# Decays of a gated recurrence as running products, scores in four pieces, and outputs with tokens in the partitions

## The reference

```python
f = lb + (1.0 - lb) * jax.nn.sigmoid(f_pre)
log_f = jnp.log(f)
k = 1.0 - f
...
def step(state, xs):
    qc, lfc, kc, vc = xs
    b = jnp.cumsum(lfc, axis=2)
    o_inter = jnp.einsum('bhtk,bhkv->bhtv', qc * jnp.exp(b), state)
    diff = b[:, :, :, None, :] - b[:, :, None, :, :]
    decay = jnp.exp(jnp.where(causal, diff, -jnp.inf))
    attn = jnp.einsum('bhtk,bhsk,bhtsk->bhts', qc, kc, decay)
    o_intra = jnp.einsum('bhts,bhsv->bhtv', attn, vc)
    b_last = b[:, :, -1, :]
    k_dec = kc * jnp.exp(b_last[:, :, None, :] - b)
    new_state = jnp.exp(b_last)[..., None] * state + jnp.einsum('bhsk,bhsv->bhkv', k_dec, vc)
    return new_state, o_inter + o_intra
...
o = rms_norm(o, hgrn_norm_w[l]) * jax.nn.silu(heads(g_h, HGRN_HEAD_V))
```

## Time and profile before

| | before |
|---|---|
| median of 3 runs | 1179.38 us (1178.89 to 1179.52) |
| the profiled execution: time, span | 1178.28 us, 1176.5 us |
| PE busy | 1125.3 us, 96% |
| DVE, ACT, POOL busy | 73%, 47%, 14% |
| granted clock of PE, mean | 0.99 |
| DMA, mean | 116 GB/s |

### The profile page before, as it was taken

How to read it: one execution, slowest core, us unless ns; L and a number is a source line. 1 busy time by engine, 2 the same in 40 slices (tenths; PEclk the granted TensorE clock), 3 DMA queues, 4 the chain that set the end, 5 groups by cost and what they waited for, 6 DMA issues and landing times.

```text
span 1176.5 us, 15092 instructions
## 1 busy us (share of the span) xinstructions
PE 1125.3 (96%) x5995; PEld 902.4 (77%) x5995; DVE 859.3 (73%) x1348; ACT 554.4 (47%) x857; POOL 164.6 (14%) x179
## 2 busy tenths in 40 slices
PE   4889999999999999999999999999999999999996
PEld 3667777777788878888886766778888888888885
DVE  5879899999867784666788799786765666655246
ACT  3574555544622343776425676546544434341130
POOL 1044443334423210000100000200000000000001
PEclk9899999999999999999999999999999999999999
DMA  9642323323524566313110022112333233243201
GB/s 376 250 179 99 117 77 139 143 74 142 172 88 171 204 260 233 116 64 121 52 38 37 1 72 72 36 72 72 108 108 103 77 108 106 79 158 141 91 17 71
DMA packets 22654, 136.66 MB, mean 116 GB/s; under 512 B 2576, under 2 KB 2872, under 8 KB 8760
## 3 DMA queue, kind: packets, MB, share of 16 engines
q1 hardware_dynamic: 19936, 128.46, 30.0%
q10 hardware_dynamic: 2648, 7.25, 1.8%
HBM read 133.58 MB, written 2.12 MB: 115 GB/s over the span
## 4 chain that ended last, share of the span: by engine, by line
PE 68%; DVE 18%; ACT 6%; issue 3%; POOL 3%; DMA 2%; DVEq 0%; SPq 0%; ACTq 0%; POOLq 0%
PE PB L185 67%; DVE WL L206 3%; DVE RAW L1412 3%; ACT WH L199 2%; DVE AT L234 1%; DVE UPA L206 1%; DVE SS L214 1%; POOL UPA L206 1%; POOL PTA L206 1%; DVE PTA L206 1%; DVE MPH L1412 1%; DVE XL L214 1%; DMA XL<-in_x 1%; DMA RAW<-in_wstream 1%; DVE HB L231 1%
## 5 line engine op out<-in xcount | busy, mean ns | idle before, releaser
L185 PE MATMUL PB<-HH,WH 128*128 128x512 f32 (+1 forms) x896 | 352.9, 394 | 12.1 <-DVE HL L206 7.4
L185 PE MATMUL PB<-HH,WL 128*128 128x512 f32 (+1 forms) x896 | 340.7, 380 | 0.0
L185 PE MATMUL PB<-HL,WH 128*128 128x512 f32 (+1 forms) x896 | 340.4, 380 | 0.0
L206 DVE TENSOR_TENSOR WL<-RAW,WH 128x1024 fp32r<-128x1024 f32 (+2 forms) x172 | 205.5, 1201 | 178.9 <-ACT WH L199 178.6
L199 ACT ACTIVATE WH<-RAW 128x1024 fp32r<-128x1024 f32 (+2 forms) x172 | 167.4, 979 | 290.9 <-PE PB L185 265.3
L185 PEld LDWEIGHTS PB<-HH,WH 128*128 128x128 f32 x896 | 169.3, 189 | 49.8 <-DVE HL L206 8.4
L185 PEld LDWEIGHTS PB<-HH,WL 128*128 128x128 f32 x896 | 169.4, 189 | 32.9
L185 PEld LDWEIGHTS PB<-HL,WH 128*128 128x128 f32 x896 | 169.7, 189 | 28.6 <-issue 0.5
L214 DVE SCALAR_TENSOR_TENSOR CV<-VP,PC,CV 128x512 f32<-128x512 f32 x120 | 88.1, 778 | 0.7
L206 POOL TENSOR_TENSOR PX<-PX,NPOW 128x2 f32<-128x2 f32 (+2 forms) x7 | 6.5, 935 | 461.2 <-DVE PX L206 422.8
L185 PE MATMUL PB<-WH,AH 128*128 128x512 f32 x176 | 68.5, 389 | 0.0
(11 more groups left out here) (283 smaller groups left out, 1789.3 us busy)
## 6 DMA issues: line engine op xcount, KB each, us to landing
RAW<-in_wstream SPq DMA_DIRECT2D x101, 1024.0 KB, 4.9
EARLY<-in_wstream SPq DMA_DIRECT2D x7, 1024.0 KB, 15.8
RAW<-in_wstream SPq DMA_DIRECT2D x5, 768.0 KB, 4.5
RAW<-in_wstream SPq DMA_DIRECT2D x5, 512.0 KB, 3.6
XL<-in_x SPq DMA_DIRECT2D x2, 1024.0 KB, 8.5
HB<-in_x SPq DMA_DIRECT2D x2, 1024.0 KB, 6.3
out<-XL SPq DMA_DIRECT2D x8, 256.0 KB, 2.0
ROWS<-in_rows ACTq DMA_DIRECT2D x3, 512.0 KB, 8.1
```

The costliest lines, as they stand in the source:

```text
L185: return self.put(lambda e: e.matmul(o, l, r, start=start, stop=stop, skip_group_check=skip))
L206: return self.put(lambda e: e.tensor_tensor(o, a, b, op))
```

## The change

No logarithm, scan or exponential is left. ACT makes both f (into Bb) and k (into Kb) from the sigmoid with two linear activations (`gates`). The decays are built up level by level, in place: `Kb` and a working copy of the queries `QM` (Qb times f; two buffers, the former Q0 and E0) hold the decays within blocks of 2^(l-1) tokens; DVE's `up(l)` multiplies the earlier halves of Kb by the gate product of the later half, and the later halves of QM by that of the earlier half, two instructions of 256 columns. POOL makes those products of 2, 4, ... 64 gates by pairs (`total`, into TOT: 256, 128, ... 8 columns). ACT copies, at each level, the early halves of Kb and the late halves of QM into EW[l-1] (two instructions). So level l+1 can't be made before level l was copied. Scores of a level have only the 32 late tokens of each chunk as columns, and two levels share a bank and a tick: level 0 at step -3, levels 1 and 2 at step 1, 3 and 4 at step 3, 5 and 6 at step 5. After level 6 Kb and QM are the fully decayed keys and queries, used by `kt` (step 6) and `qs`. Values are turned over at step -6 instead of 0, KDT is copied by ACT at step 7, `o` and `kv` move to step 8. The output has tokens in the partitions: AT and QM are stationary, Vb and SS move; the `qs` products have 128x64 stationary tiles and 128 columns, even and odd chunks in other halves of the partitions. The square sums come from ACT's accumulator, four squares of 128 columns (step 13), so `st` on PE is gone; `dg` now multiplies XT by DG in four products of 128 columns, which scales and turns the head back, and one DVE instruction multiplies by weight and output gate. The four-instruction diagonal, the state chain, the masks and everything after the recurrence stay.

```diff
+    QM = [Q0[:, :], E0[:, :]]
...
+    PIECE = (0, 1, 1, 2, 2, 3, 3)
+
+    def totals(h, l):
+
+        if l == 1:
+            return head_bufs(h)[2]
+        if l == 7:
+            return TOT[:, 496 + 8 * (h % 2):504 + 8 * (h % 2)]
+        return TOT[:, 512 - (1024 >> (l - 1)):512 - (512 >> (l - 1))]
+
+    def pairs_of(h, l):
+        return totals(h, l).rearrange("p (n b) -> p n b", b=2)
...
-        def ew(h, l):
-            half, blk = 1 << (l - 1), 1 << l
-            Bb = head_bufs(h)[2]
-            x = ew_buf(h, l - 1)
-            Bv, Xv = halves_of(l, Bb, x)
-            ref = Bv[:, :, half - 1:half].broadcast_to([128, 512 // blk, half])
-            g.wait_ge(S_.v_s, ("b", h))
-            if ew_before(h, l - 1):
-                g.wait_ge(S_.p_sm, ew_before(h, l - 1))
-            g.tt(Xv[:, :, half:blk], Bv[:, :, half:blk], ref, SUB)
-            g.tt(Xv[:, :, 0:half], ref, Bv[:, :, 0:half], SUB).then_inc(S_.g_s, ("ew", h, l))
+        def total(h, l):
+
+            f = pairs_of(h, l - 1)
+            if l == 2:
+                g.wait_ge(S_.a_s, ("k", h))
+                if h:
+                    g.wait_ge(S_.v_s, ("uq", h - 1, 7))
+            else:
+                g.wait_ge(S_.g_s, ("tot", h, l - 1))
+            if l == 7 and h > 1:
+                g.wait_ge(S_.v_s, ("ss", h - 2))
+            g.tt(totals(h, l), f[:, :, 0:1].rearrange("p n b -> p (n b)"), f[:, :, 1:2].rearrange("p n b -> p (n b)"), MUL)\
+                .then_inc(S_.g_s, ("tot", h, l))
 
         def hgrn(h, step):
             Vb, Kb, Bb, Qb, Gb = head_bufs(h)
-            if step == -1:
+            if step == -7:
+                for l in (2, 3, 4):
+                    total(h, l)
+            elif step == -6:
+                for l in (5, 6, 7):
+                    total(h, l)
+            elif step == -5:
                 clear(h)
-            if step < 0:
-                ew(h, step + 7)
-            elif step == 3:
-                x = ew_buf(h, 6)
-                Bv, Xv = halves_of(6, Bb, x)
-                g.wait_ge(S_.p_sm, ew_before(h, 6))
-                g.tt(Xv, Bv[:, :, 63:64].broadcast_to([128, 8, 64]), Bv, SUB).then_inc(S_.g_s, ("kd", h))
             elif step == 14:
                 sc = sct(h % 2)
-                g.wait_ge(S_.v_ax, ("st", h))
+                g.wait_ge(S_.v_s, ("st", h))
                 power(sc[:, 4:8], sc[:, 0:4], 4, ("pow", h))
-            elif step == 22:
-                g.wait_ge(S_.v_ax, ("dg", h))
-                g.wait_ge(S_.a_ev, ("z", h, 3))
-                g.tt(XT[:, h, :], XT[:, h, :], Gb, MUL).then_inc(S_.g_s, ("oh", h))
...
-            if step < 0:
-                x = ew_buf(h, step + 6)
-                a.wait_ge(S_.g_s, ("ew", h, step + 7))
-                a.act(x, x, ACTF.Exp).then_inc(S_.a_s, ("ew", h, step + 7))
-            elif step == 3:
-                a.wait_ge(S_.v_s, ("b", h))
+            if -3 <= step < 3:
+                l = step + 4
+                half, blk = 1 << (l - 1), 1 << l
+                Kv, Qv, Xv = halves_of(l, Kb, QM[h % 2], EW[l - 1])
                 if h:
-                    a.wait_ge(S_.v_s, ("ss", h - 1))
-                a.act(E0[:, :], Bb, ACTF.Exp).then_inc(S_.a_s, ("e0", h))
-                x = ew_buf(h, 6)
-                a.wait_ge(S_.g_s, ("kd", h))
-                a.act(x, x, ACTF.Exp).then_inc(S_.a_s, ("kd", h))
+                    a.wait_ge(S_.p_sm, ("sc", h - 1, PIECE[l]))
+                a.wait_ge(*((S_.v_s, ("uk", h, l)) if l > 1 else (S_.a_s, ("k", h))))
+                a.copy(Xv[:, :, 0:half], Kv[:, :, 0:half]).then_inc(S_.a_s, ("xk", h, l))
+                a.wait_ge(S_.v_s, ("uq", h, l))
+                a.copy(Xv[:, :, half:blk], Qv[:, :, half:blk]).then_inc(S_.a_s, ("xq", h, l))
+            elif step == 7:
+                a.wait_ge(S_.p_sm, ("kt", h))
+                if h:
+                    a.wait_ge(S_.p_sm, ("kv", h - 1))
+                a.copy(KDT[:, :], aux.of(("kt", h))).then_inc(S_.a_ax, ("kt", h))
             elif step == 13:
                 a.wait_ge(S_.p_sm, ("qs", h))
                 a.wait_ge(S_.v_h, ("h", 7))
                 a.copy(XT[:, h, :], aux.of(("o", h)))
-                a.wait_ge(S_.v_s, ("b", min(h + 1, 7)))
-                a.act(XR[3], aux.of(("o", h)), ACTF.Square).then_inc(S_.a_ax, ("o", h))
+                for j in range(4):
+                    op = a.act(XR[3][:, js(j)], aux.of(("o", h))[:, js(j)], ACTF.Square, acc=sct(h % 2)[:, 8 + j:9 + j])
+                op.then_inc(S_.a_ax, ("o", h))
...
+            a.act(Kb, main.of(("z", h, 1)), ACTF.Sigmoid).then_inc(S_.a_ev, ("z", h, 1))
+            a.wait_ge(S_.v_s, "lb")
+            a.wait_ge(S_.a_ev, ("z", h, 1))
+            a.act(Bb, Kb, ACTF.Identity, bias=LB[:, h:h + 1], scale=OML[:, h:h + 1])
+            a.act(Kb, Kb, ACTF.Identity, bias=OML[:, h:h + 1], scale=LT[:, h:h + 1]).then_inc(S_.a_s, ("k", h))
...
-        def head(h, b):
-            Vb, Kb, Bb, Qb, Gb = head_bufs(h)
-            if b == 1:
-                v.wait_ge(S_.a_ev, ("z", h, 1))
-                v.wait_ge(S_.v_s, "lb")
-                v.ts(Kb, Kb, OML[:, h:h + 1], LB[:, h:h + 1], MUL, ADD).then_inc(S_.v_s, ("f", h))
-                v.wait_ge(S_.a_s, ("ln", h))
-                v.ts(Kb, Kb, -1.0, 1.0, MUL, ADD).then_inc(S_.v_s, ("k", h))
-                if h > 1:
-                    v.wait_ge(S_.a_s, ("kd", h - 2))
-                v.scan(Bb, SM[:, :], XR[3]).then_inc(S_.v_s, ("b", h))
-
         def hgrn(h, step):
             Vb, Kb, Bb, Qb, Gb = head_bufs(h)
-
-            def ew(l):
-                half, blk = 1 << (l - 1), 1 << l
-                Kv, Qv, Xv = halves_of(l, Kb, Qb, ew_buf(h, l - 1))
-                v.wait_ge(S_.a_s, ("ew", h, l))
-                v.wait_ge(S_.a_ev, ("z", h, 2))
-                v.wait_ge(S_.v_s, ("k", h))
-                v.tt(Xv[:, :, half:blk], Xv[:, :, half:blk], Qv[:, :, half:blk], MUL)
-                v.tt(Xv[:, :, 0:half], Xv[:, :, 0:half], Kv[:, :, 0:half], MUL).then_inc(S_.v_s, ("ew", h, l))
+            Qm = QM[h % 2]
+
+            def up(l):
+
+                half, blk = 1 << (l - 2), 1 << (l - 1)
+                Kv, Qv = halves_of(l - 1, Kb, Qm)
+                f = pairs_of(h, l - 1)
+                n = 512 // blk
+                if l == 2:
+                    v.wait_ge(S_.p_sm, ("sc", h, 0))
+                else:
+                    v.wait_ge(S_.g_s, ("tot", h, l - 1))
+                    v.wait_ge(S_.v_s, ("uq", h, l - 1))
+                v.wait_ge(S_.a_s, ("xk", h, l - 1))
+                v.tt(Kv[:, :, 0:half], Kv[:, :, 0:half], f[:, :, 1:2].broadcast_to([128, n, half]), MUL).then_inc(S_.v_s, ("uk", h, l))
+                v.wait_ge(S_.a_s, ("xq", h, l - 1))
+                v.tt(Qv[:, :, half:blk], Qv[:, :, half:blk], f[:, :, 0:1].broadcast_to([128, n, half]), MUL)\
+                    .then_inc(S_.v_s, ("uq", h, l))
...
+                v.where(o, m, d).then_inc(S_.v_ax, ("in", h, l), *[("sc", h, PIECE[l])] * (l % 2 == 0))
+
+            if step == -3:
+                v.wait_ge(S_.a_s, ("k", h))
+                v.wait_ge(S_.a_ev, ("z", h, 2))
+                if h > 1:
+                    v.wait_ge(S_.p_sm, ("qs", h - 2))
+                v.tt(Qm, Qb, Bb, MUL).then_inc(S_.v_s, ("uq", h, 1))
+            if -2 <= step < 4:
+                up(step + 4)
+            if step == -1:
+                sc(0)
+            elif step in (2, 4, 6):
                 sc(step - 1)
-            if step == 3:
-                v.wait_ge(S_.a_s, ("e0", h))
-                v.wait_ge(*((S_.p_sm, ("qs", h - 1)) if h else (S_.v_h, ("h", 7))))
-                v.tt(Q0[:, :], E0[:, :], Qb, MUL).then_inc(S_.v_s, ("q0", h))
-                x = ew_buf(h, 6)
-                v.wait_ge(S_.a_s, ("kd", h))
-                v.tt(x, x, Kb, MUL).then_inc(S_.v_s, ("kd", h))
...
+                        op = v.stt(SS[:, c, :], SS[:, c - 1, :], totals(h, 7)[:, c:c + 1], kv, MUL, ADD)
...
-                v.wait_ge(S_.a_ax, ("o", h))
-                v.stt(XT[:, h, :], XT[:, h, :], col("hgrn_norm_w"), aux.of(("dg", h)), MUL, MUL)\
+                v.wait_ge(S_.a_ev, ("z", h, 3))
+                v.stt(XT[:, h, :], aux.of(("dg", h)), col("hgrn_norm_w"), Gb, MUL, MUL)\
...
+            def sc(bk, l, at, n):
+
+                half, blk = (0, 64) if l == 0 else (1 << (l - 1), 1 << l)
+                k, q = (Kb, Qb) if l == 0 else (EW[l - 1], EW[l - 1])
                 for c in range(8):
                     cs, rs = slice(64 * c, 64 * c + 64), slice(64 * (c % 2), 64 * (c % 2) + 64)
-                    op = pe.mm(bk[rs, cs], (Kb if l == 0 else x)[:, cs], (Qb if l == 0 else x)[:, cs], True, True)
-                op.then_inc(S_.p_sm, ("sc", h, l))
-
-            if step == 0:
...
+            elif step == -3:
+                bk = take_aux(("sc", h, 0))
+                pe.wait_ge(S_.a_s, ("k", h))
+                pe.wait_ge(S_.a_ev, ("z", h, 2))
```

(34 more changed lines are left out.)

107 lines of the change are left out of this document (29 added, 78 removed).

## The result

| | before | after |
|---|---|---|
| median of 4 runs each | 1179.14 us (1178.57 to 1179.52) | 1146.58 us (1143.33 to 1147.24) |
| profiled execution: time, span | 1178.28, 1176.5 | 1147.24, 1145.4 |
| ratio | | 0.9719, 95% interval 0.970 to 0.9738 |
| head length, mean of six, from one head's `dg` to the next | 35.57 us | 31.98 us |
| DVE, POOL busy in a head | 34.2 of 36, 14.4 | 26.7 of 32, 5.3 |

A forecast was written before the change was run, and what follows sets the result against it. PE, busy 96% of the span, was taken as the bound, DVE as second limit. Savings 22.5 + 9.6 + 6.2 less waits 2.5 + 2.1 gave 33.7 us off 1178.28; adjusted to the median, forecast 1146 us, range 1134 to 1160.

The forecast's parts named there:

- Square sums: On PE, per head: the `st` piece goes, saving 0.81 us.
- SS products: On PE, per head: 14 passes with 64-wide tiles fall from 1.58 to 1.09 us, saving 0.49; bounds 0.54 and 1.72.
- `dg`: On PE, per head: 1.05 us becomes 8 passes like `o`, 0.98, saving 0.07.
- Six score pieces at 0.465: On PE, per head: 32 columns instead of 64 cut each piece from 0.62 to 0.465 us, saving 0.93.
- Interruptions, three fewer at 0.17: PE's projection, per head: small pieces at 8 ticks instead of 11, 0.17 us each, saving 0.51.
- Gaps of heads 1 to 7: PE's gaps from DVE's lateness, 9.6 us in all, go as DVE and POOL get less work.
- Wait (b): PE, next head's level 0 at step -3: waits 0.35 us behind ACT's copy and squares, 2.5 us for seven heads.
- Wait (a): PE at step 3, serial chain of levels: no wait for level 4 while DVE's lag is under 6.7 us.
- Wait (c): Head 0: PE comes to levels 1 and 2 about 2.1 us early; against 6.2 lost before, nets 4.1.
- The rival of the small products: PE's scores and SS products don't get cheaper, a floor of tile loading rules: 1158 us, chance 0.15.
- The rival of the moved gaps: DVE's lag stays at 8.4 and PE waits at step 3, or squares take their upper bound: 1156 to 1158 us, chance 0.15.

The follow-up runs named there:

- run 6: Kernel before, with DVE's f, k, scan, Q0 and decayed keys of every head cut from 512 columns to 8: 1168.41 us.
- run 4: Changed kernel with the square sums back on PE at step 14, in a tick of their own: 1152.56 us.
- run 3: Changed kernel with full 128x128 stationary tiles for the SS products instead of 128x64 tiles in alternate halves: 1149.78 us.
- run 5: Kernel before, with POOL's differences of Bb for heads 1 to 7 cut to 8 columns, DVE's instructions kept: 1168.43 us.
- run 1: Changed kernel with 64 columns instead of 32 in the score products of levels 1 to 6: 1145.84 us.
- run 8: Changed kernel with levels 1 to 6 each at a tick of its own instead of in three pairs: 1154.77 us.
- run 7: Changed kernel with 16 dummy differences of 224 columns a head added on POOL: 1162.26 us.
- run 9: Changed kernel with ACT's and DVE's level work of head 0 put ahead of later splits, before the second head: 1144.51 us.
- run 2: Changed kernel with 16 columns instead of 32 in the score products of levels 1 to 6: 1145.97 us.
- run 10: Changed kernel with values turned over at step -8 and levels 5 and 6 at step 6, two interruptions fewer a head: 1144.78 us.

## Why the prediction was right, and where it wasn't

The total is right, and so are the two main causes, work on PE and DVE's lag. Several terms are not as sized, and the closeness of the total (1145.7 and 1146.58) is partly luck: two misses of some 6 us cancel, and the four executions of the changed kernel alone lie 4 us apart. What is called measured here takes the kernel before without its stalls, from run 6.

1. **Square sums**, 0.81 with its interruption 0.98: 0.94 measured in run 4.
2. **SS products**, 1.09 forecast by the `kv` row: 1.02. The upper bound of 1.72 was too high as well (1.48 in run 3). The saving, 0.49 forecast, is 0.37: the 1.58 us before held 0.11 of stall, and the 128x64 tiles cost 0.09 on the way in.
3. **`dg`**, 0.98 forecast: 0.98 (96.45 to 97.43 in the trace of after). The 1.05 before was no floor: in runs 5 and 6 it is 0.95, so nothing was saved.
4. **Six score pieces at 0.465**: wrong. The columns give 0.03 us for a lone piece (0.62 to 0.59), 0.18 a head and not 0.93, and 0.08 a head in pairs by run 1. The row `kv` with twice the columns suggested proportion; the row `st` with its high floor at one column was the better guide, and I took the middle between them.
5. **Interruptions, three fewer at 0.17**: 0.51 a head forecast, 1.19 measured. They are one `st` less (0.13 by run 4), three pieces put beside another (1.06 by run 8), and one more, for the values, whose cost is made up by the time that they and level 0 take less apart. Terms 4 and 5 were 1.44 us a head together; measured they are 0.18 + 1.06 + 0.13 = 1.37. The misses are 6.0 us too much in term 4 and 5.4 too little in term 5 for 8 heads, and the two errors came from one: part of what an interruption costs was booked as the piece's. The 0.135 us ahead of `dg` (170.78 to 172.39) was in part a stall as well: in run 6 `dg` starts 0.24 after the last product.
6. **Gaps of heads 1 to 7**, 9.6 forecast: 12 by run 6's floor, 10 by run 5's. POOL at 5 us a head: 5.3. DVE at 27.5: 26.7; its lag 2.5 instead of 4. The stretch of DVE by POOL, 4 us a head by estimate, is 3.8 in run 5.
7. **Wait (b)** behind the squares, 0.35: 0.21, since a square with its read takes 0.25 us (four from 121.04 to 122.04). **Wait (a)**: none at a lag of 2.5; run 7 puts the limit at some 6.2, forecast 6.7. **Wait (c)**, 2.1: 2.46, and in the profiled execution nine products at the lower clock, 1.6 more, which the forecast left out; head 0 gives some 3 us instead of 4.1.

By rows, the work is 0.94 + 0.37 - 0.03 + 1.37 - 0.13 - 0.21 = 2.31 us a head (the 0.13 stands in the first term too), against 2.22 between the heads of run 6 and the changed kernel. Against the forecast 20.0 us of work net of wait (b), 9.6 and 4.1 stand 17.8, 12.1 and 3.0. The rival of the small products was right in its mechanism for the scores and wrong in what it would cost, since grouping gave in time what columns did not. The rival of the moved gaps needs only load on POOL, which run 7 shows with somewhat more than POOL had before, and so the POOL work that the change drops is not a side effect: without it up to half of the gain is gone.

## What to carry to other kernels

Where PE runs a long stream of large products, look at how its small float32 products are grouped, not at how many columns they have. Here a score piece put beside another saved 0.35 us, and going from 64 to 32 columns 0.01 to 0.03; other interruptions were worth less (0.13 for the square sums, under 0.1 for transposes and for a pair put ahead of them), so price each by its own rows. Take the kernel before without its stalls as the measure: rows beside a late engine held stalls that no bracket showed. When a queue is full to its last microsecond, look at what its neighbour does to it as well as at its own list: on this kernel each microsecond of POOL's elementwise work cost DVE 0.3 to 0.4. And when a producer is moved by a tick, move what it feeds in the consumer's queue too: one diagonal behind a dot product and a split cost 8 us.

## What the runs showed of the hardware

At two places PE's clock falls in some executions and not in others. One is head 0, shown under run 9. The other, where the program of the changed kernel and of run 1 is the same, is behind 3.5 us of one-column products in the second block (32 passes from 720.9). The stretch right after them in the profiled execution of the changed kernel, and then in that of run 1:

```profile
725.00:730.00 5.00, 5.00 (x13) 3.94 (x13) 3.95 (x16) 2.41 (x3) 1.33 (x1) 0.50 0.00 0
```

```profile
725.00:730.00 5.00, 5.00 (x23) 4.12 (x22) 4.04 (x16) 2.50 (x3) 1.33 (x1) 1.00 0.00 0
```

At 0.50, 1.2 GHz, a product takes 0.43 us instead of 0.23, and the products until the clock is back cost 3 us there; in the profiles of runs 2, 3, 4, 9 and 10 about half as many are slow. Executions of one kernel differ accordingly: the changed kernel took 1143.33 us at a mean clock of 0.994 and 1146.56 to 1147.24 at 0.990, and runs 1, 4 and 6 show two groups some 3 us apart too. That the falls are what parts them is shown for the profiled executions only, since the others have no trace. Differences of the size of runs 1, 2, 9 and 10 can't be read from a median of four.
